# Modulation rows turned by a two-column selection product instead of eight transposes and a reduction, with ten filler products on TensorE ahead of the filter products

## The reference, cut to what matters

```
def modulation(cond, l):
    return jax.nn.silu(cond) @ w_mod[l] + b_mod[l]

def layer(x, l, mod, mixer):
    sh1, sc1, g1, sh2, sc2, g2 = jnp.split(mod, N_MOD, axis=-1)
    y, aux = mixer(_rmsnorm(x, norm_mix[l]) * (1.0 + sc1) + sh1)
    x = x + g1 * y
    h = _rmsnorm(x, norm_ffn[l]) * (1.0 + sc2) + sh2
    x = x + g2 * _moe(h, router_w, router_bias, w_gate, w_up, w_down)
```

## Time and profile before

| | |
|---|---|
| median of 3 runs | 898.97 us (898.81 to 905.19) |
| the profiled execution | 898.81 us, span 897.0 us |
| mean granted TensorE clock | 0.945 |
| busy in the span: PE, PEld, DVE, ACT, POOL | 89%, 50%, 40%, 31%, 12% |

### The profile page before, as it was taken

One profiled execution on the slowest core, in us unless ns is written; L12 is line 12 of the kernel. 1 busy time (PEld: TensorE's weight loads), 2 busy tenths in 40 slices (PEclk: granted clock), 3 DMA queues, 4 the chain that ended last, 5 costly groups with the idle time before them and its releaser, 6 DMA issues.

```text
span 897.0 us, 11721 instructions
## 1 busy us (share of the span) xinstructions
PE 794.1 (89%) x4159; PEld 452.5 (50%) x4159; DVE 362.2 (40%) x836; ACT 278.8 (31%) x648; POOL 107.9 (12%) x153
## 2 busy tenths in 40 slices
PE   7899999999789997999885898888899989999860
PEld 3358755435334564555453555555544655555430
DVE  6660642650443442422116356466532423321114
ACT  1751122212530342222215356556521521222111
POOL 1400000011000013010122020220200130000120
PEclk9989999999889988999997999999999969999995
DMA  8992332399913388999979980220147579999965
GB/s 285 365 345 75 113 125 97 114 348 280 363 79 102 128 316 270 407 411 411 408 280 315 331 308 30 96 95 3 49 138 285 194 252 332 406 411 410 374 228 214
DMA packets 84183, 219.56 MB, mean 245 GB/s; under 512 B 9527, under 2 KB 19392, under 8 KB 83806
## 3 DMA queue, kind: packets, MB, share of 16 engines
q1 hardware_dynamic: 73822, 197.89, 60.7%
q0 software_dynamic: 8800, 17.38, 5.8%
q10 hardware_dynamic: 1504, 3.56, 1.0%
HBM read 214.18 MB, written 14.83 MB: 255 GB/s over the span
## 4 chain that ended last, share of the span: by engine, by line
PE 67%; DMA 11%; DVE 9%; ACT 4%; SPq 4%; issue 3%; DVEq 2%; ACTq 0%; POOL 0%; POOLq 0%
PE ps L946 59%; PE ps L953 4%; DMA arena<-in_moe_w_up_dram 4%; PE ps L1184 2%; DVEq L1981 2%; DMA hT<-h_rows,row_now 2%; SPq L658 2%; DMA xn<-y_rows 2%; DMA x<-in_x_sample_dram 2%; DVE negmax L2049 1%; DMA hT<-h_rows,rows_in 1%; SPq L675 1%; SPq L705 1%; PE ps L1198 1%; DVE xn L2447 1%
## 5 line engine op out<-in xcount | busy, mean ns | idle before, releaser
L946 PE MATMUL ps<-arena 128*64 128x256 f32 (+11 forms) x1164 | 229.3, 440 | 14.4 <-DMA arena<-in_moe_w_up_dram 4.9
L946 PEld LDWEIGHTS ps<-arena 128*64 128x64 f32 (+3 forms) x1164 | 125.5, 165 | 100.1 <-issue 58.7
L946 PE MATMUL ps<-ring,hT 128*128 128x512 f32 (+2 forms) x384 | 133.3, 508 | 4.5 <-issue 3.9
L946 PE MATMUL ps<-ring,arena 128*64 128x256 f32 (+1 forms) x784 | 111.3, 431 | 5.1 <-DMA ring<-in_moe_w_down_dram 3.5
L946 PEld LDWEIGHTS ps<-ring,hT 128*128 128x128 f32 x384 | 73.3, 192 | 62.6 <-issue 58.1
L946 PEld LDWEIGHTS ps<-ring,arena 128*64 128x64 f32 x784 | 53.9, 137 | 51.0 <-issue 27.7
L1634 ACT ACTIVATE arena<-ps 128x256 f32<-128x256 f32 (+4 forms) x94 | 42.3, 463 | 86.8 <-PE ps L946 83.0
L953 PE MATMUL ps<-ident,arena 128*128 128x128 f32 (+2 forms) x332 | 50.6, 290 | 17.4 <-DVE hT L2055 4.6
L946 PE MATMUL ps<-hT,ring 128*128 128x384 f32 x192 | 62.1, 486 | 0.0
L2381 DVE TENSOR_TENSOR arena<-arena,ps 128x128 f32<-128x128 f32 x37 | 10.7, 288 | 123.3 <-ACT arena L1742 123.3
L953 PEld LDWEIGHTS ps<-ident,arena 128*128 128x128 f32 (+2 forms) x332 | 38.7, 140 | 38.4 <-issue 13.9
(11 more groups left out here) (314 smaller groups left out, 859.4 us busy)
## 6 DMA issues: line engine op xcount, KB each, us to landing
ring<-in_w_mod_dram SPq DMA_DIRECT2D x48, 1024.0 KB, 8.9
ring<-in_moe_w_down_dram SPq DMA_DIRECT2D x22, 1024.0 KB, 17.6
ring<-in_moe_w_gate_dram SPq DMA_DIRECT2D x38, 512.0 KB, 15.0
ring<-in_moe_w_up_dram SPq DMA_DIRECT2D x38, 512.0 KB, 16.5
arena<-in_moe_w_gate_dram SPq DMA_DIRECT2D x36, 512.0 KB, 6.9
arena<-in_moe_w_up_dram SPq DMA_DIRECT2D x36, 512.0 KB, 7.7
arena<-in_moe_w_down_dram SPq DMA_DIRECT2D x15, 1024.0 KB, 9.6
ring<-in_ev_w_in_dram SPq DMA_DIRECT2D x9, 1024.0 KB, 15.8
```

The source lines that it names most:

```text
L946: mm = pe.matmul(out, lhsT, rhs, **kw)
```

## The change

`mod_turn` no longer transposes. For each of the eight strided slices of the row it makes a product with the 64 columns of the slice as weights and a two-column selector, `rowsel[:, :, 0]`, as the moving side. The sum over g happens in the product, the result is 64 x 2 for each slice, at partitions 64*half on, all eight side by side in sixteen columns of one bank. So each of the four modT stages claims one bank in place of two, and DVE's `mod_add` is one add that reads PSUM. Ten filler products of 128x128 are put ahead of the first filter product. The order of the work on the engines is otherwise the same, but the rotating pointer is four banks behind from the opening's hT0.0 stage on.

```
-WARM_FIRST, WARM_SIN = 10, 8
+WARM_FIRST, WARM_SIN, WARM_FILT = 10, 8, 10
...
-    B.stage("modT0", 2)
+    B.stage("modT0", 1)
...
-    B.stage("modT1", 2)
+    B.stage("modT1", 1)
...
-    B.stage("modT2", 2)
-    B.stage("modT3", 2)
+    B.stage("modT2", 1)
+    B.stage("modT3", 1)
...
+                bank = claim(f"modT{i}")
                 drained_wait(pe, f"mod{l}.{v}.{half}")
-                for part in range(2):
-                    bank = claim(f"modT{i}", part)
-                    for j in range(4):
-                        mm = pe.transpose(bank[0:64, P * j:P * j + P], row[:, 4 * part + j::KT], ident[:, :])
-                    fill_inc(mm, f"modT{i}", part)
+                for j in range(KT):
+                    mm = product(bank[64 * half:64 * half + 64, 2 * j:2 * j + 2], row[:, j::KT], rowsel[:, :, 0], carries=False, start=True, stop=True)
+                fill_inc(mm, f"modT{i}")
...
                         if od == 0 and t == 0 and r == 0:
+                            warm(bank, WARM_FILT)
                             pe.wait_ge(w3_ready, 2)
...
                     if where == "start" and i >= 2:
-                        filled_wait(act, f"modT{i - 2}", 1)
+                        filled_wait(act, f"modT{i - 2}")
...
-                total = turned_sum[rows].rearrange("p (j c) -> p j c", c=2)
-                for part in range(2):
-                    bank = filled_wait(dve, f"modT{i}", part)
-                    groups = bank[0:64, :].rearrange("p (j g k) -> p j k g", g=4, k=32)[:, :, 0:2, :]
-                    drain_inc(dve.tensor_reduce(total[:, 4 * part:4 * part + 4, :], groups, AXX, ALU.add), f"modT{i}", part)
-                settle()
-                dve.tensor_tensor(modT[rows, l, v, :, :], total, modT[rows, l, v, :, :], ALU.add)
+                bank = filled_wait(dve, f"modT{i}")
+                turned = bank[rows, 0:2 * KT].rearrange("p (j c) -> p j c", c=2)
+                drain_inc(dve.tensor_tensor(modT[rows, l, v, :, :], turned, modT[rows, l, v, :, :], ALU.add), f"modT{i}")
                 mod_scale(l, v, half)
```

More of the change, by code:

```diff
@@ L469, in build_step @@
         conv_scaled = gb[:, 1, 848:912].rearrange("p (g k m) -> p g k m", g=2, k=4)
-        turned_sum = gb[:, 1, 912:928]
         modbias = gb[:, 1, HY + P:HY + P + 12 * KT].rearrange("p (l v j) -> p l v j", l=2, j=KT)
```

## The result

The changed kernel takes 909.70 us (median of 8 runs, 905.63 to 911.99) against 899.23 us for the kernel before in the same comparison (8 runs, 898.81 to 905.19): ratio 1.0109, interval 1.0080 to 1.0139. Neither interval holds 1, so it is slower, by about 0.95%, 8.5 us, and the forecast of 902.5 us with its range to 906.5 was wrong. The profiled execution took 908.2 us, span 906.4 us, at a mean granted clock of 0.942 (0.945 before).

The account below looks back on a forecast made before the run. The prediction took TensorE's stream to bound the kernel. It summed -0.3 us (opening), +2.5 (Hyena banks) and +1.5 (clock fall) to +3.7 us on 898.81 us, so 902.5 us, with a range of 898.5 to 906.5.

Parts of the forecast that it names:

- -0.3 us (-0.9 to +0.2): Whole opening up to `energies(1)`: turns +0.2, earlier start of the roots -0.24, shorter add on DVE -0.28.
- is carried to the end: Behind the Hyena stage everything hangs on TensorE's stream, so the shift of +3.7 us reaches the kernel's end.
- the fall of the clock behind 200: Hyena stage: after the new 2.8 us idle time the clock falls to half in most executions, +1.5 us (0 to 3.4).
- The turn's price: Opening, TensorE: a turn is 16 records at 0.071 us each, 1.13 us at full clock, 2.27 at half as upper ends.
- Cost nothing, covered by chunk 3's two DMA waits.: Opening: the filler delays filters through chunk 2 by 1.3 us, swallowed by chunk 3's waits of 0.57 and 2.00 us.
- The clock behind the turns: End of the opening: turns 2 and 3 run at half clock, 4.0 us taken (3.4 to 4.5) in place of 3.8.
- rival (b): The opening keeps its clock, `energies(1)` 1.85 us earlier: 901.0 us, or 899.5 with no clock fall at 200; chance 0.20.
- The DVE term: DVE after turn 3: a reduction and a drain go, so the sums `energies(1)` waits for come earlier, -0.28 us.
- The roots' term: Opening, TensorE: `root_turn(0)` no longer waits for a DVE copy and starts right behind chunk 3, -0.24 us.
- The Hyena stage: New bank waits: 2.85 us before chunk 4 for DVE, 0.86 before `inv1` for ACT, 0.65 before chunk 6 gone; +2.5 net.

Follow-up runs that it names:

- after_again: The changed kernel unaltered, profiled and timed a second time against the kernel before: 909.56 us, ratio 1.0081.
- e5: The changed kernel without the ten filler products and with the old banks from the input projection on, so the new turns alone: 909.98 us, ratio 1.0082.
- e8: e5 with each product's weights 64 neighbouring columns instead of every eighth element; one execution, only the opening read: turn 0 took 1.09 us.
- e3: The kernel before with only the ten filler products added ahead of the first filter product: 904.12 us, ratio 1.0028.
- e4: The changed kernel without the ten filler products, new turns and new banks kept: 914.66 us, ratio 1.0121 against the kernel before.
- e9: e5 with each product moving 64 selector columns in place of two: 908.84 us, ratio 1.0048 against the kernel before.
- d5: The kernel before with 5 more filler products behind `energies(1)`, a delay of 1.1 us: ratio 1.0003.
- d15: The kernel before with 15 more filler products behind `energies(1)`, a delay of 3.4 us: ratio 1.0076.
- d30: The kernel before with 30 more filler products behind `energies(1)`, a delay of 6.7 us: ratio 1.0057.
- e1: The kernel before with the rotating bank pointer moved by four ahead of the input projection, old turns and no new filler: 907.83 us, ratio 1.0045.
- e6: The kernel before with the rotating bank pointer moved by one ahead of the input projection: 902.98 us, ratio 0.9996.
- e2: The changed kernel with the old banks restored from the input projection on, new turns and filler kept: 905.76 us, ratio 1.0030 against the kernel before.

## Why the prediction was wrong

Two steps failed. The first is the opening, put as "-0.3 us (-0.9 to +0.2)": it measured +1.8 us in the profile after and +2.2 in `after_again` (`energies(1)` at 54.40 and 54.81), +2.2 for the turn alone (e5). The second is that the shift "is carried to the end": it is, and more comes on top. In the two profiles of the changed kernel chunk 6 is 4.2 and 4.6 us late, only half a microsecond to one more than the +3.7 of the forecast. That is luck: the opening was 2.1 to 2.5 us worse, and the fall of the clock behind 200, booked with 1.5 us, stayed out. At the end the times say 8.5 us. So most of the miss lies behind chunk 6. With the opening as measured and all else as forecast the sum would have been 904.6 to 905.0 us, inside the range.

In the opening, all of the loss arises ahead of the roots: they start 1.74 us late, and from there to `energies(1)` it is 8.50 us in the profile after against 8.45. Three points in it were off.

- **The turn's price**, "0.071 us each". The row of 24 records had weights that lie side by side; the weights here are every eighth element of the row. At 0.13 us a record a turn is 2.08 us and not 1.13. Shown by e8. I had looked for a row with the right width and count and not for one with the right access pattern, though `row[:, j::KT]` stood in the diff. My bounds (0.052 to 0.071) came from one row and left this out. For turns 2 and 3 the number came out all the same, by luck: 3.5 us, inside "3.4 to 4.5", since they ran at full clock and not at half.
- **"Cost nothing, covered by chunk 3's two DMA waits."** This is the step that cost the time. The filler alone is covered, and e3 shows it: 0.47 us of wait are left. But I charged it 1.3 us of delay where the profile after has 3.11, since it ran partly at a clock of 0.50 (0.71 over 17.2 to 20.4) and began at 17.18; and turns 0 and 1, which I booked as nothing since they lie before the same waits, add 1 us each. 3.1 + 2.1 is over 2.57: chunk 2 starts at 42.33, 5.4 us late, and chunk 3 ends 2.05 us late. In `after_again` the filler delays the filters by 1.67 us only, and the clock's fall behind turn 0 adds 1.8. The mistake is to have held each delay against the cover and never their sum. The point at which the cover is used up was in the prediction ("early or late by less than 2.57 us").
- **The clock behind the turns.** I took turns 2 and 3 to run at half clock as before. In the profile after they ran at full clock (3.5 us together) and the 24 transposes behind them mostly at half (4.29 us against 3.39). In the pair e4 and e9 the clock fell behind the stretch with two columns and not behind the one with 64. The 0.9 us lost in the transposes were made up by the wait for DVE that is gone (0.41 us) and by the roots and the taps, which ran at full clock (0.80 us up to turn 2 against 1.22), so this point moved the sum little. This was rival (b) turned round: I had weighed that filler and products keep the clock up, with the Trainium skill's rule that transposes don't count as work for it ("TensorE: Matmul & The Clock Gate", section "Part 4: PE-mode transpose"). The profile after doesn't bear the rule out: from 50.2 TensorE ran transposes alone, and from 53.2 the clock was at 1.00. That the opening can keep its clock at all is seen in the kernel before: in d5, d15 and d30, which change nothing ahead of `energies(1)`, it stayed at 1.00 over 43 to 51, and `energies(1)` came at 51.14 to 51.69. So the old opening scatters by 1.5 us (51.14 to 52.61), and the new one starts above it (54.40 to 56.01 with two columns).

The DVE term was right. From the end of turn 3 to the sums it was 0.91 us and is 0.65 us now (turn 3 ends at 50.25; timeline of DVE, kernel after):

```profile
50.28 0.18 DVE L2005 TENSOR_TENSOR modT<-ps,modT 64x16 f32<-64x16 f32 x1 [1.30 <-PE ps L945]
...
50.90 1.22 DVE L2516 TENSOR_TENSOR arena<-arena 128x1024 f32<-128x1024 f32 x1
```

It bought nothing, as `energies(1)` has no wait for DVE any more: TensorE itself comes to it late. The roots' term was right too (no wait at 45.90), and it counts: chunk 3 ends 2.05 us late, the roots start 1.74 late.

**The Hyena stage was right** in place, releaser and size: 2.78 for 2.85, 0.89 for 0.86, chunk 6 without its 0.65. Chunk 6 is 2.44 us later than the opening's shift explains (4.23 - 1.79); forecast 2.5. The fall of the clock behind 200, +1.5 us, wasn't in the profiled execution of after, nor in `after_again` (`inv1` there is 151.57 us behind `energies(1)`, in the profile after 151.60), but it was in e1 and in e4 (half over 202.5 to 206). Two of the four profiles with the wait had it, at 1.4 to 1.7 us, so some 0.8 us would have been the better mean, with both outcomes as likely in any one profile.

**"The shift is carried to the end"** holds up to chunk 6 in every kernel, and d5 to d30 are consistent with it behind chunk 6. But the change does more than shift: the three longer waits for DVE, 1.0 us in all and at least 0.7 after what comes back, belong to it and stand in no row of the prediction, which counted the shorter `mod_add` as a gain of 0.28 us and nothing else. In the profile after, the third store of `h_rows` adds some more: the gather behind it starts 2.80 us after DVE wrote its rows (L2278 ends at 341.25), in `after_again` 0.94 us after it (342.38, 343.32), so the late store cost 1.9 us. That is not the change's doing: the store stands in the chain in five profiles, with 9.86 us (after), 10.31 (e4), 8.34 (e6), 7.69 (d15) and 7.46 (e1), and e6 and d15 have the old turns and fillers of the kernel before. Why it lands late is argued and not shown: SP issued three weight pieces just around it in the profile after, and a microsecond later in e1.

**What stays open.** Opening 2.2 us, banks 2.4 (waits alone) to 4.1 (e1, with the fall of the clock) and DVE's waits 0.7 to 1.0 make 5.3 to 7.3 us; the two comparisons measured 9.8 (7.2 to 12.5) and 7.3 (4.5 to 10.1) of a kernel of 900 us. The second agrees with the sum, the first only at its edge. The experiments don't add up neatly either: e5, the turn alone, is at 1.0082, and e2, the turn and the filler, at 1.0030, with hardly overlapping intervals, though e2's `energies(1)` is half a microsecond later than e5's. e4, e5 and e9 lose 3.5 to 5.2 us more by the times than chunk 6 is late in their profiles, of which DVE's waits are at most 1. Whether the rest is scatter from where the clock falls, or the new turn has further effects behind chunk 6, isn't settled, nor whether the filler gives something back there. No kernel here beats the one before.

## What to carry to other kernels

Add up all delays in front of one meeting point before calling any of them covered: a wait can be spent once. Price a small product by a row with the same access pattern of its weights, not only the same shape, and look at the granted clock behind it and not only at its length. When a stage claims fewer buffers from a rotating pool, follow the pool to the next place where it meets fixed ones; that was worth about half of this change's loss, 150 us behind the edited code, and the order of the instructions shows it before any run. After an edit that changes the number of instructions on an engine, compare that engine's gaps far behind the edit too. And profile the kernel before twice: its own tail moved by 3 us. Several profiles of each side then separate what is the same in all of one side from what scatters.

## What the hardware showed that I had not expected

- **Stride in fp32 weights.** Sixteen records with 64-column weights: 1.09 us when the columns are neighbours, 2.08 us when they stand 8 elements apart (e8, after), each at clock 1.00. The strided transposes of before took 1.04 us for 8 records, also 0.13 us a record. Whether that was the stride's price too (they move 128 columns each) no run shows; that a product leaves twice the records and pays it on each does.
- **Columns and the clock.** Turns of 2 and of 64 columns take 2.08 and 2.13 us at 100% busy, and the clock fell to 0.50 behind the first and not behind the second, at two places in one pair of kernels (e4, e9). Over all five profiles with two columns it fell behind turn 0 in four and behind turns 2 and 3 in five. For 64 columns it is one profile, and e9's own span was no shorter for it than e5's (908.4 against 906.2 us).
- **A gap on DVE that goes by the count.** With 12 DVE records fewer, instructions number 319, 447, 831 and 1087 start 0.35 us later after the one before them than in the old kernels, in six profiles of six, and in none of nine with the old count.
- **A store among weights.** The same store of `h_rows` took 7.46 us in e1, 9.86 us in the profile after and 10.31 us in e4.
